# Interleaving the two head groups of a gated delta rule, and laying the first layer's projections over its attention stages

## What is computed

```python
# first block
z = rms_norm(x, attn_norm_g) @ w_in            # columns: lat (416), dq, dk, dv (512 each)
y_mla  = mla_group(...)    # 8 heads; q, k from the latent part, norm per head and rope; softmax over 512 keys
y_diff = diff_group(...)   # 4 heads x 2 maps: q = rms_norm(dq), k = rms_norm(dk); softmax(a) - lam*softmax(b); out norm
x = x + concat(y_mla, y_diff) @ w_out
x = x + conv_ffn(rms_norm(x, ffn_norm_g), ...)
# second block, inside the token mixer: gated delta rule, 8 heads, chunks of rows in order
A = tril_strict((k*beta) @ k.T * decay);  solve (I + A) [u, w] = [v*beta, k*beta*exp(G)]
per chunk: v_new = u - w @ state;  o = q_dec @ state + qk @ v_new;  state = state*g_last + k_tail.T @ v_new
o = rms_norm(o) * silu(z)
```

## Time and profile before

| | |
|---|---|
| median of 3 runs | 2770.85 us (2769.6 to 2771.02) |
| the profiled execution: its own time | 2766.78 us |
| its span, first to last instruction | 2764.8 us |
| PE busy | 2361.8 us (85%) |
| DVE busy | 1014.5 us (37%) |
| ACT busy | 459.8 us (17%) |
| POOL busy | 119.9 us (4%) |
| mean granted TensorE clock | 0.921 |

### The profile page before, as it was taken

The page is one execution under the profiler, slowest core; times in us unless marked ns, Lnnn a source line. Parts: engine busy times, 40 slices in busy tenths (PEclk is TensorE's granted clock), DMA queues, the critical chain, the costliest instruction groups (busy, mean ns, idle before and its releaser), DMA issues.

```text
span 2764.8 us, 21616 instructions
## 1 busy us (share of the span) xinstructions
PE 2361.8 (85%) x7941; PEld 1185.7 (43%) x7941; DVE 1014.5 (37%) x1900; ACT 459.8 (17%) x922; POOL 119.9 (4%) x110
## 2 busy tenths in 40 slices
PE   5977667899999988898997789777999969999883
PEld 3433343444444434344446654575444533343321
DVE  3056663322220032277575649454011542222113
ACT  0013431000000000104233324242000100000002
POOL 0000000000000000000002100111000000000000
PEclk9988857999999999999998899988999979999997
DMA  5245200121222202210010001000313269999995
GB/s 197 95 149 191 72 1 20 50 91 61 76 76 84 69 31 81 61 61 31 31 61 31 1 25 68 31 1 1 99 70 148 96 261 426 426 427 426 426 426 206
DMA packets 95536, 358.22 MB, mean 130 GB/s; under 512 B 10325, under 2 KB 19074, under 8 KB 82882
## 3 DMA queue, kind: packets, MB, share of 16 engines
q1 hardware_dynamic: 85121, 336.42, 31.3%
q0 software_dynamic: 8192, 18.79, 1.8%
q10 hardware_dynamic: 2112, 1.57, 0.2%
HBM read 352.81 MB, written 15.47 MB: 133 GB/s over the span
## 4 chain that ended last, share of the span: by engine, by line
PE 71%; DVE 15%; ACT 5%; DMA 5%; issue 3%; SPq 0%; DVEq 0%; ACTq 0%; POOLq 0%
PE bank L572 46%; PE bank L1068 7%; PE bank L813 5%; PE bank L915 5%; DMA mem<-in_w_up 4%; PE bank L591 3%; ACT mem L1778 3%; DVE mem L1491 2%; PE bank L716 1%; PE bank L630 1%; DMA mem<-in_conv_w 1%; PE bank L1048 1%; DVE mem L1152 1%; DVE mem L1151 1%; ACT L1889 1%
## 5 line engine op out<-in xcount | busy, mean ns | idle before, releaser
L572 PE MATMUL bank<-mem 128*128 128x512 f32 (+8 forms) x3488 | 1461.7, 583 | 60.0 <-ACT mem L1778 14.2
L572 PEld LDWEIGHTS bank<-mem 128*128 128x128 f32 (+2 forms) x3488 | 657.1, 199 | 824.2 <-issue 745.5
L1068 PE MATMUL bank<-mem 128*64 128x512 f32 x1248 | 284.9, 612 | 31.4 <-DMA mem<-in_w_up 16.6
L591 PE MATMUL bank<-mem 128*128 128x128 f32 (+1 forms) x820 | 166.6, 332 | 157.9 <-DVE mem L1152 33.2
L1778 ACT ACTIVATE mem<-bank 128x256 f32<-128x256 f32 (+5 forms) x381 | 177.9, 467 | 650.9 <-PE bank L591 278.5
L915 PE MATMUL bank<-mem 128*128 128x128 f32 x1344 | 208.6, 305 | 61.7 <-DVE mem L1525 34.5
L915 PEld LDWEIGHTS bank<-mem 128*128 128x128 f32 x1344 | 187.5, 214 | 76.3 <-DVE mem L1525 36.7
L591 PEld LDWEIGHTS bank<-mem 128*128 128x128 f32 (+1 forms) x820 | 113.6, 167 | 218.4 <-DVE mem L1152 37.5
L1068 PEld LDWEIGHTS bank<-mem 128*64 128x64 f32 x1248 | 92.8, 140 | 213.8 <-issue 202.4
L813 PE MATMUL bank<-mem 128*128 128x512 f32 x352 | 151.6, 592 | 0.9 <-DVE mem L1391 0.9
L1988 POOL TENSOR_TENSOR mem<-mem 128x512 f32<-128x512 f32 x48 | 64.2, 1344 | 1305.5 <-ACT mem L1778 1208.3
(11 more groups left out here) (278 smaller groups left out, 1354.8 us busy)
## 6 DMA issues: line engine op xcount, KB each, us to landing
mem<-in_w_gate SPq DMA_DIRECT2D x37, 2048.0 KB, 23.1
mem<-in_w_up SPq DMA_DIRECT2D x37, 2048.0 KB, 24.5
mem<-in_w_down SPq DMA_DIRECT2D x36, 2048.0 KB, 25.8
mem<-in_w_in SPq DMA_DIRECT2D x18, 2048.0 KB, 7.8
mem<-in_w_ada SPq DMA_DIRECT2D x12, 2048.0 KB, 8.0
mem<-in_w_out SPq DMA_DIRECT2D x4, 2048.0 KB, 7.7
mem<-in_w_ple_gate SPq DMA_DIRECT2D x2, 2048.0 KB, 7.7
mem<-in_w_br_att SPq DMA_DIRECT2D x2, 2048.0 KB, 8.4
```

What stands on the lines that cost most here:

```text
L572: last = pe.matmul(o, l, r, start=(i == 0), stop=(i == len(pairs) - 1))
L591: last = pe.transpose(b[0:width, i * P:(i + 1) * P], s, ident)
L1068: last_ = pe.matmul(o[here, :], lhs[:, k, here], w[:, k, cols], start=(k == 0), stop=(k == kk - 1))
```

## The change

It does these things:

- **Projections.** Only `lat` and blocks 0 and 1 of `dq` stay ahead of the expansion; the other ten blocks (dq 2, 3, dk, dv) lie between the expansion and the head turns of stage 2 (`project`, three per block q and one in the last). The modulation blocks move: 0 and 1 to the end of stage 2, 2 to 9 one per head of MLA, 10 and 11 into differential attention.
- **dq and dk norms.** The eight norms of stage 4 are done by DVE in stage 2, behind the heads of each block (2, 3, 3). Their turning is one per head in MLA. The bias is loaded and scaled inside MLA. MLA's q goes to the place of x (`mla_qT`), and x is loaded again from its input after MLA.
- **Differential attention** goes block after block (q outer, head inner). Out norm, turning, `w_out` product, addition to x, norm of x and its turning for block q follow four to twelve turns behind, inside the same loop (`group_at`).
- **Delta rule.** The projections of both groups come first. Then one loop over `DELTA_ORDER`: 17 steps a chunk, the second group 9 steps behind the first, each level with all four heads at once. Products with the zero state of chunk 0 (k_bg, q with state, w with state) and the last chunk's state update are left out, for both groups. Buffers lie in x's place (x is written to DRAM and read back) and, for group 1, in weight slots 2 and 0; so the loads of items `br_a` and later wait until the delta loop has ended.

The core of the diff:

```diff
+STEPS, LAG = 17, 9
+def delta_order():
+    for at in range(STEPS * NT + 4 + LAG):
+        for g in range(2):
+            ch, step = divmod(at - LAG * g, STEPS)
+            if 0 <= ch < NT or ch == NT and step < (4 if g == 0 else 3):
+                yield g, ch, step
 # PE, stage 2
-            expand(0)
+            beside = ((("dq", 2), ("dq", 3), ("dk", 0)), (("dk", 1), ("dk", 2), ("dk", 3)),
+                      (("dv", 0), ("dv", 1), ("dv", 2)))
+            for q in range(NT - 1):
+                expand(q)
+                project(*beside[q][0])
                 head_turns(8, QK)
+                project(*beside[q][1])
                 head_turns(8, QK)
+                project(*beside[q][2])
 # DVE, stage 2, behind the k heads of block q
+                for name, r in beside_norms[q]:
+                    dve.wait_ge(act_free, mark[name, r])
+                    v = S1[name][:, r, :].rearrange("p (g d) -> p g d", g=8)
+                    norm_heads(v, v, 8, 64, rows(f"diff_{name[1]}_norm_g"), square, diff_rows)
 # PE, differential attention
-        diff_units = [(h, q) for h in range(DIFF_H) for q in range(NT)]
+        diff_units = [(h, q) for q in range(NT) for h in range(DIFF_H)]
+            for n in DIFF_TURNS:
                 ...
+                q = group_at(n, 2)
+                if q is not None:
+                    out_turned(q)
+                q = group_at(n, 7)
+                if q is not None:
+                    x_turned(q)
+                for c in range(2):
+                    q = group_at(n, 3 + c)
+                    if q is not None:
+                        out_product(q, c)
 # PE, delta rule: a step of one group
+                elif step < 14 and step % 2 == 0:
+                    lv = step // 2 - 1
+                    if lv == 0:
+                        to_wait(x0_ready[g])
+                    to_wait(level_ready[g])
+                    if lv:
+                        pe.wait_ge(dve_free, updated[g])
+                        turn("act", [B["X"][:, h, :] for h in range(HG)])
+                    four("act", lambda h: B[f"L{lv % 2}"][:, h, :], lambda h: B["X"][:, h, :])
                     ...
+                elif step < 14:
+                    pe.wait_ge(act_free, turned_at[g])
+                    if lv < 5:
+                        four("dve", lambda h: B["XT"][:, h, :], lambda h: B["u"][:, h, :])
 # DVE, delta rule
+                if step == 0:
+                    V(tt(B["A"], full_bank(), B["decay"], ALU.mult), dve_free)
+                    V(tt(B["A"], B["A"], inner(beta[:, ch, gh], P), ALU.mult), a_ready[g])
+                elif step == 1:
                     V(tt(B["X"], B["A"], over(const("level0"), HG), ALU.mult))
                     V(tt(B["X"], over(ident, HG), B["X"], ALU.subtract))
                     dve.wait_ge(act_free, mark["AT", g, ch])
                     V(tt(B["XT"], B["AT"], over(const("level0_t"), HG), ALU.mult))
+                    V(tt(B["XT"], over(ident, HG), B["XT"], ALU.subtract), x0_ready[g])
 # SP
+                if n == FIRST_GATE + 1:
+                    sp.wait_ge(dve_free, mark["delta", 1, NT - 1])
```

More of the change, by code:

```diff
@@ L893, in _, with four, gains_along_rows @@
                       lambda b, h: b[:, :], S3["pT"])
+            def four(ring_name, lhs, rhs):
+                b = bank(ring_name)
+                for h in range(HG):
+                    last = pe.matmul(b[:, h * P:(h + 1) * P], lhs(h), rhs(h), start=True, stop=True)
+                full(last, ring_name)
+            def gains_along_rows(g):
+                to_wait(decay_in[g])
+                four("dve", lambda h: delta[g]["tmp"][:, h, :], lambda h: const("upper"))
             for g in range(2):
@@ L906, in _ @@
                             b = bank("act")
-                            full(product(b[:, :], [(const("ones"), flat(S4[("tmp", "decay")[i % 2]]))]), "act")
-                by_token("act", weights("z")[0], hT, 512)
-                used("act")
-                B = S4
-                def some(ring_name, heads_, lhs, rhs):
-                    b = bank(ring_name)
-                    for i, h in enumerate(heads_):
-                        last = pe.matmul(b[:, i * P:(i + 1) * P], lhs(h), rhs(h), start=True, stop=True)
-                    full(last, ring_name)
@@ new lines, in _, with delta_step @@
+                w = weights("z")[0]
+                for q in range(NT):
+                    if g and q >= 2:
+                        gains_along_rows(q - 2)
+                    b = bank("act")
+                    full(product(b[:, :], [(hT[:, k, q * P:(q + 1) * P], w[:, k, :]) for k in range(KD)]), "act")
+                used("act")
+            turned_at, updated = {}, {}
+            def delta_step(g, ch, step):
+                B = delta[g]
+                cs = slice(ch * P, (ch + 1) * P)
+                q_, k_, v_ = (lambda h, n=n: S4[n][:, g * HG + h, cs] for n in "qkv")
+                if ch == NT:
+                    if step == 3:
+                        result_turned(g, ch)
+                    return
+                if step == 0:
+                    four("dve", k_, k_)
+                elif step == 1:
+                    to_wait(a_ready[g])
@@ L976, in _, with result_turned @@
+            def result_turned(g, ch):
+                to_wait(result_ready[g])
+                turn("act", [delta[g]["result"][:, h, :] for h in range(HG)])
+                mark["result", g, ch - 1] = done["act"]
+            pe.wait_ge(silu_out, FT + 24)
+            for g, ch, step in DELTA_ORDER:
+                delta_step(g, ch, step)
             taken("dve")
             for c in range(2):
-                by_feature("act", weights("gate_a")[0], hT, 4)
+                w = weights("gate_a")[0]
+                for m in range(4):
+                    b = bank("act")
+                    full(product(b[:, :], [(w[:, k, m * P:(m + 1) * P], hT[:, k, :]) for k in range(KD)]), "act")
+                    if c == 0 and m == 0:
+                        result_turned(1, NT)
@@ L1888, in _ @@
                         if part:
[L1889 removed]
+                            C(act.activation(flat(delta[0][("tmp", "decay")[i % 2]]), take()[:, :], ACT.Sqrt,
                                              bias=eps_col), act_free)
```

675 lines of the change are left out of this document (399 added, 276 removed).

## The result

The changed kernel takes **2604.81 us** (median of 4 runs, 2604.74 to 2611.39) against 2770.93 for the one before: a ratio of 0.9407, 95% interval 0.939 to 0.9423. The forecast was 2591, the range 2545 to 2640. Its profiled execution took 2604.84 us, its span 2603.0, 161.8 less than before.

A forecast was written before the change was run, and what follows sets the result against it. First-layer stages were either full on PE with DVE idle or hung on DVE and ACT; the delta loop ran twice. Gains 106 + 74 = 180 from 2766.78 give 2586.8, plus 4.07 for the median: 2591 us, range 2545 to 2640.

The forecast's parts named there:

- the two places named: First layer, with a gain of 106 us, and the delta loop, with a gain of 74 us.
- Stage 2: Stage 2 with ten projection blocks and eight norms laid in: ends at 193.3 in place of 251.81, gain 58.5 us.
- MLA: MLA with modulation in four more heads and a turn in eight: 73.8 becomes 87.2 us, loss 13.4.
- The loop is PE's: In MLA, PE sets the pace: a head takes 7.60 us without modulation and 9.95 with it.
- To the feed-forward part: From MLA's end to the first feed-forward product: 196.9 becomes 136 us (101 of PE's content plus 34.5), gain 61.
- Delta rule: End of z to `gate_a`: one loop of 260 us (190 + 5.6 + 22 + 43) replaces 334.1, gain 74.
- DVE's two ordered blocks a round: Delta loop: twice a round DVE runs A, X and XT in order, 6.2 us, costing 2 x 4.2 a round.
- Masks: Delta loop: a fifth of POOL's 32 masks newly slow DVE's work, 6.5 us, counted within the 43 of waits.
- The rival's 26 on top: Delta loop: DVE becomes the bound, nearly all 32 masks hit it, 26 us more, 2617 us; chance 0.15.
- The cleaner overlap: Both loops: 30 of the delta loop's 43 us and the units' stalls of 15 go, 2546 us; chance 0.20.
- The first layer's overlay: Rival that it fails: products in PE's order delay the next unit's values, 42 us more, 2633 us; chance 0.12.
- the slower rival: PE stays at 1.2 GHz in the first layer's and the delta loop, 275 us more, 2866 us; chance 0.02.

The follow-up runs named there:

- Run 5: Changed kernel with the delta rule's second head group starting only after the first has gone through its four chunks (68 steps behind, not 9): 2700.59 us.
- Run 8: Changed kernel without the squares, their sums and the product by the inverse root in stage 2's dq and dk norms: 2605.34 us.
- run 2: Changed kernel with ACT's exponentials of MLA's next unit ahead of its copies of the modulation's sums and the turned rows: 2598.51 us.
- Run 4: Changed kernel with all but the first two POOL masks of a group made for 8 of 128 columns: 2583.1 us.
- run 3: Changed kernel with POOL's first mask of a chunk waiting until DVE has made its group's first inverse: 2599.71 us.
- run 6: Changed kernel with the delta rule's second group 4 steps behind the first in place of 9: 2598.86 us.
- run 7: Changed kernel with PE's independent delta rule work (turns of k and v, product of q and k) ahead of its waits for first inverse or updated X: 2600.1 us.
- run 11: Changed kernel with the edits of run 2, run 3, run 6 and run 7, and ACT's roots behind its copy of the turned probabilities: 2570.84 us.

## Why the prediction was right, and where its steps failed

**The mechanism and the order of size held.** 162 us of a forecast 180 came, in the two places named, by PE filling what were gaps. Run 5 shows it for the delta rule, where the groups in turn lose 95.5 us; for the first layer the windows show it. That two of the four stretches came within 4 us is in part luck, since in both of them errors cancel.

- **Stage 2: right in sum.** MLA's first score at 192.2 against 193.3; the start of the stage was 1.7 earlier (66.0), so the stretch itself was 0.6 longer than forecast. The block's size was 26.8 for PE where I had 28.0, and one block of three came near the DVE limit of 28.4, at 28.0. The three blocks took 81.8 where I had 84.8, and the fourth block with what follows it 24.1 where I had 21.7, with a wait of PE of 4.28 us for DVE's rope (L1369). Run 8 prices DVE's part at 2.4 us.
- **MLA: the loss was 21.8, not 13.4.** "The loop is PE's" failed. The step priced four more heads at 2.35 each and the turns at 0.5 each, and as a price of PE's loop that was near: run 2, with ACT's order mended, has 89.1 from the end of stage 2, of which 4.2 lie ahead of the first score by the changed kernel's rows, so some 85 for MLA against my 87.2. Its heads lie 9.7 us apart, those of the changed kernel 11.1, where I had 10.4. What I left out is that ACT's copy of the sums stands ahead of the next exponential, so that every head pays PE's sums as a wait of DVE (31.2 us in the changed kernel; 12.4 in the kernel before, with sums in four heads).
- **To the feed-forward part: 143.6 against 136.** The idle time was right as a sum, 33.9 against 34.5, but not in its parts: ACT's root stalls took 13.9 where I had 6 (three times 2), because in two of the three ACT first waits for squares that stand behind the out norm on DVE. PE's own time was 109.7 where the sum had 101. By the prediction's own way of counting (busy time times granted clock) 109.7 at 0.88 is 96.5, so the content was not too small. What failed is that the sum took it at the full clock.
- **Delta rule: 263.8 against 260.** Idle 64.1 where I had 70; of that DVE's two ordered blocks a round are 26.4 us in eight waits of 3.3, where I had 2 x 4.2 a round, 29.4; the waits for A (L1684), 10.4 us with the one at the head, come on top. PE's own time was 199.7 against 190, at 0.94, and again it is the clock that the sum left out (199.7 x 0.94 = 188). The two errors, 6 less and 10 more, nearly cancel.
- **Masks.** I had 6.5 us of new collisions. DVE's extra time is L1642 3.7, L1620 3.1, L1619 1.6 and L1640 0.7: 9.1. The rival's 26 on top did not come. Run 4 puts nearly all of the masks' cost, old and new, at 26.7, the time that PE waits for a mask itself included.
- **The rivals.** The cleaner overlap did not come; runs 3, 6 and 7 show that it was there to be had by other orders. The first layer's overlay did not fail: the loop is 7.6 us over the forecast, not 42, and PE's waits for DVE's shares in it (L1464) are 5.7 us in six. The lower clock that the slower rival named is there only in part: the granted 0.88 and 0.94 are means of stretches at 2.4 GHz and shorter ones at 1.2 GHz, where that rival had 1.2 GHz throughout.

The Trainium skill (GPSIMD Engine Reference, Specifications) names two kinds of VectorE instructions that contend with GpSimd: those with two SBUF inputs and those in a 2-port perf mode. The trace agrees for the first kind: L1689, L1690 and L1642 are slower beside a mask, and L1704, with one operand in a bank, is not. L1620 reads one tile and constants and is slowed too, 947 ns on the mean and 429 in run 4. By the page it would have to be of the second kind, which no row of a trace names.

## What to carry to other kernels

When work is laid into a loop, read the order of the engine that only copies: a copy that waits for the new work must not stand ahead of the step that feeds the loop (10.7 us in MLA, some 5 to 7 with the loop behind it). Price PE's content in a loop that still has gaps at the clock that such gaps leave (0.83 to 0.94 here), not at the full one. Taking many gaps away can give clock back (interleaving: 60.6 us of idle, and 34.9 of PE's own time), and taking a few away need not: in runs 7 and 11 idle time fell by 9.7 and 5.2 us, and PE's own grew by 3.1 and 1.7. And judge an edit by its own stretch, and by the sum with the stretch beside it, against a run whose clock ahead of it was the same.

## What was not expected of the hardware

The clock of an untouched loop took one of three patterns (about 0.88, 0.85 and 0.83; 143.6 to 148.9 us). They went with the length of the stretch ahead of it and repeated within 0.2 us among the profiled executions of one pattern, and the same code was seen in two of them. With 10.7 us taken out of MLA, the loop behind it was 5.2 longer.

An instruction of DVE of 128 x 4 elements is slowed beside POOL's masks by nearly as much as a large one. L1619 takes 0.16 us by itself and took 0.99 in run 3, while POOL made five masks from 1551.71 on. It stands here with the next instruction, a TENSOR_SCALAR of 128x512 that takes 0.43 by itself:

```profile
1553.24 0.99 DVE L1619 TENSOR_TENSOR mem<-mem 128x4 f32<-128x4 f32 x1
...
1554.27 1.46 DVE L1620 TENSOR_SCALAR mem<-mem 128x512 f32<-128x512 f32 x1
```
